# A rewritten last mixer and five smaller edits at the seams of a two-block transformer kernel (one core)

## The reference

```python
# first block, twice: feed-forward, mixer, feed-forward (272 rows: 16 meta tokens and 256 tokens)
def token_mixer(h, ...):
    fq, fk, fv, ff, gq, gk, gv, ga, gr, g_merge_a, g_merge_b = jnp.split(h @ w_in, points, axis=-1)
    o_fox = fox_attention(heads(fq), heads(fk), heads(fv), log_f, key_valid)      # 8 heads of 64
    log_a = log_sigmoid(ga @ w_alpha_up + b_alpha) * (valid / 16)
    o_gla = gla_chunked(heads(gq) / 8, heads(gk), heads(gv), heads(log_a))        # 4 heads
    o_gla = rmsnorm(o_gla, g_gla_out) * silu(gr)
    y = sigmoid(g_merge_a) * (o_fox @ w_fox_o) + sigmoid(g_merge_b) * (o_gla @ w_gla_o)
    return y @ w_out
# after the first block only the 256 tokens go on: first_block returns h[:, BLOCK:]

# second block: ffn, mlstm_mixer, ffn; k_sh, v_sh; ffn, dilated_mixer, ffn
def dilated_mixer(h, mem_n, k_sh, v_sh, w_q, q_gain, w_out, rel_bias, w_mem_kv, ...):
    p = h @ w_q                                            # 12 heads of 64, and 4 memory heads
    q_d = rms_norm(heads(p[..., :768]), q_gain)
    for g, (window, dilation) in enumerate(((128, 1), (512, 4), (2048, 16))):   # 4 heads in each
        s = q_d[g] @ k_sh[g].T / 8 + bias[bucket of distance]; causal, in dilated windows
        outs[g], lses[g] = softmax(s) @ v_sh[g], log of the sum
    h_d = outs * softmax(lses over the three groups)
    h_m = memory_cross_attention(p[..., 768:], mem_n, w_mem_kv, ...)   # 4 heads, 256 memory rows
    return concatenate([h_d, h_m]) @ w_out
# feed-forward: x + 0.5 * ((silu(n @ w_gate) * (n @ w_up)) @ w_down), n = rms_norm(x)
```

## Time and profile before

| | us |
|---|---|
| median of 3 runs | 2573.98 (2571.54 to 2575.33) |
| the profiled execution, its time | 2574.36 |
| its span from first to last instruction | 2573.0 |
| PE busy | 2448.4 (95%), mean granted clock 0.967 |
| DVE busy | 1676.7 (65%) |
| ACT busy | 1246.6 (48%) |
| DMA | 385.85 MB, mean 150 GB/s |

### The profile page before, as it was taken

One profiled execution on the slowest core, in us unless ns is written; L12 is line 12 of the kernel. 1 busy time (PEld: TensorE's weight loads), 2 busy tenths in 40 slices (PEclk: granted clock), 3 DMA queues, 4 the chain that ended last, 5 costly groups with the idle time before them and its releaser, 6 DMA issues.

```text
span 2573.0 us, 45875 instructions
## 1 busy us (share of the span) xinstructions
PE 2448.4 (95%) x18769; PEld 2322.9 (90%) x18769; DVE 1676.7 (65%) x3006; ACT 1246.6 (48%) x2099; POOL 33.6 (1%) x63
## 2 busy tenths in 40 slices
PE   7999999999999989999999998999999999769999
PEld 6999788899999977899999998989998999457999
DVE  5656777776575487778648846756656765455664
ACT  5444455554354445556445634645445644334542
POOL 2000000000000000000000000000000000000000
PEclk9999999999999999999999998989999999677999
DMA  7655433565465453346655653427655665412653
GB/s 193 174 179 141 117 91 109 141 182 176 148 178 175 158 132 99 99 137 189 189 183 162 183 176 102 119 58 191 185 184 157 180 189 171 127 41 83 180 181 140
DMA packets 589729, 385.85 MB, mean 150 GB/s; under 512 B 44587, under 2 KB 564111, under 8 KB 589392
## 3 DMA queue, kind: packets, MB, share of 16 engines
q1 hardware_dynamic: 585408, 374.00, 50.5%
q10 hardware_dynamic: 2336, 5.92, 0.6%
q0 software_dynamic: 1776, 2.98, 0.4%
HBM read 378.59 MB, written 4.19 MB: 149 GB/s over the span
## 4 chain that ended last, share of the span: by engine, by line
PE 87%; DVE 8%; ACT 2%; issue 1%; DMA 1%; ACTq 0%; DVEq 0%
PE bank L516 86%; DVE wlo L1906 2%; DVE ry L1925 1%; DVE ry L1923 1%; PE bank L825 0%; ACT whi L1243 0%; DVE smh L2357 0%; DVE rst L1927 0%; PE bank L601 0%; ACT rst L1264 0%; DMA xs<-in_x 0%; PE bank L1163 0%; ACT rst L1266 0%; DMA wraw<-in_w_ffn_gu 0%; DVE ssb L2677 0%
## 5 line engine op out<-in xcount | busy, mean ns | idle before, releaser
L1906 DVE TENSOR_TENSOR wlo<-wraw,whi 128x1024 fp32r<-128x1024 f32 (+2 forms) x723 | 866.7, 1205 | 290.7 <-ACT whi L1243 287.3
L1243 ACT ACTIVATE whi<-wraw 128x1024 fp32r<-128x1024 f32 (+2 forms) x723 | 746.9, 1042 | 596.5 <-DMA wraw<-in_w_ffn_gu 175.2
L516 PE MATMUL bank<-xhi,whi 128*128 128x256 f32 (+2 forms) x4024 | 606.6, 291 | 40.7 <-ACT xhi L1279 24.6
L516 PE MATMUL bank<-xhi,wlo 128*128 128x256 f32 (+2 forms) x4024 | 592.8, 287 | 11.4 <-DVE wlo L1906 11.4
L516 PEld LDWEIGHTS bank<-xhi,whi 128*128 128x128 f32 (+1 forms) x4024 | 535.4, 190 | 63.0 <-ACT xhi L1279 27.1
L516 PE MATMUL bank<-xlo,whi 128*128 128x256 f32 (+2 forms) x4024 | 581.4, 285 | 0.0
L516 PEld LDWEIGHTS bank<-xhi,wlo 128*128 128x128 f32 (+1 forms) x4024 | 535.5, 190 | 15.4 <-DVE wlo L1906 15.1
L516 PEld LDWEIGHTS bank<-xlo,whi 128*128 128x128 f32 (+1 forms) x4024 | 528.2, 188 | 0.2
L516 PE MATMUL bank<-act_hi,wlo 128*128 128x256 f32 (+1 forms) x1408 | 400.5, 284 | 0.0
L516 PE MATMUL bank<-act_lo,whi 128*128 128x256 f32 (+1 forms) x1408 | 400.1, 284 | 0.0
L516 PE MATMUL bank<-act_hi,whi 128*128 128x256 f32 (+1 forms) x1408 | 399.1, 283 | 0.0
(11 more groups left out here) (396 smaller groups left out, 1815.9 us busy)
## 6 DMA issues: line engine op xcount, KB each, us to landing
wraw<-in_w_ffn_gu SPq DMA_DIRECT2D x176, 512.0 KB, 3.9
wraw<-in_w_ffn_down SPq DMA_DIRECT2D x88, 512.0 KB, 3.2
wraw<-in_ffn_w_gate SPq DMA_DIRECT2D x88, 512.0 KB, 3.9
wraw<-in_ffn_w_up SPq DMA_DIRECT2D x88, 512.0 KB, 3.9
...
```

Source lines behind the costliest of these rows:

```text
L516: return E.matmul(out_, lhsT, rhs, start=first, stop=last, skip_group_check=True)
L1243: A.activation(flat(whi, u), flat(wraw, u), ACT.Copy).then_inc(S("hi"), 1)
L1906: V.tensor_tensor(flat(wlo, u), flat(wraw, u), flat(whi, u).bitcast(F32), ALU.subtract).then_inc(lo_ready[u % RING], 1)
```

## The change

1. **Fourth slab's low part**: DVE makes the wlo of the next stage's fourth slab before the additions of the last two tiles, in ffn 4, 5 and 6 and in the last mixer.
2. **Banks**: slabs 7 to 20 of mixer1 take banks 0, 1, 4, 5 in turn (`MIX_BANKS`) instead of 0 and 1; mixer2a has 6 banks of its own for its first slabs instead of 4, and its first cell step moves from step 5 to 6.
3. **Second layer's columns**: in mixer1(1), fq, gr, ma and the fo and go products are done for the 256 token columns alone, and `fox` has 16 units (queries 16 to 143 over 144 keys, 144 to 271 over 272) instead of 24.
4. **Gate bias on ACT**: ACT adds `b_alpha` as it reads the bank (Identity with bias), where DVE did; the factor 1/16 moves from a DVE multiplication into the scale of ACT's exponentials.
5. **shared_kv**: ffn 6's first `xhi` waits for the second pass of the last kv slab, not for ffn 6's own first slab.
6. **Last mixer rewritten**: the bias rows are 3 matmuls of 4x512 inside ffn 6 (steps 4, 6, 8) and 3 writes of 8 KB; the 12 reads of `bias` (128 KB each, POOL's queue, now with an overlapping source) are issued there too, and so are the memory operands `b_mp` (steps 12 to 19). Queries of the dilated heads are stored with each 128 columns reversed, which fits the reads' order; the values' operand is turned back by the product below. Slabs: 4 in the head, then bq and mkv slabs mixed; norms trail by two steps; one dilated unit per step from step 4, one memory unit per step from step 10. PE no longer transposes DVE's scaled probabilities: it multiplies the unscaled ones by a diagonal matrix that ACT makes of 1/den (`dgb`, `dgm`). The first 6 of 8 channel tiles of the first 4 output slabs are done in steps 15 to 18 while memory units run, the rest after.

```diff
+GATE_TEMP = 16.0
+MIX_FIRST, MIX_WIDE = 7, 21
+MIX_BANKS = [i if i < MIX_FIRST else (0, 1, 4, 5)[(i - MIX_FIRST) % 4] if i < MIX_WIDE else i % 2 for i in range(41)]
+B_HEAD = [("bq", 0, s) for s in (0, 2, 4, 1)]
+B_ORDER = [("bq", 0, 3), ("bq", 0, 5), ("mkv", 1, 0), ("bq", 0, 6), ("mkv", 1, 1), ("bq", 0, 7), ("mkv", 1, 2), ("mkv", 1, 3)]
+B_UNIT_STEP, B_MEM_STEP, B_TURN_STEP = 4, 10, 11
+B_IDLE, B_EARLY = 5, 4
+B_ROW_AT = (4, 6, 8)
...
-            src = IN["scratch"][h].rearrange("p u -> (p u)")[0:P * 511].rearrange("(p u) -> p u", u=511)[:, 127:127 + T]
-            G.dma_start(bias[:, h, :], src).then_inc(S("bias_in"), 16)
+            row = IN["scratch"][h, 0:1, :]
+            G.dma_start(bias[:, h, :], bass.AP(row.tensor, row.offset, [[1, P], [1, T]])).then_inc(S("bias_in"), 16)
...
 # PE, ffn
+                if F == 6 and j in B_ROW_AT:
...
+                    mm(bank[6][0:4, :], tab[0:BUCKETS + 1, 4 * g:4 * g + 4], ohb[0:BUCKETS + 1, 512 * g:512 * g + 512], True, True).then_inc(S("b_row"), 1)
 # PE, mixer1
-                    project((name, L, s), x)
+                    project((name, L, s), xq if name == "fq" else x)
 # PE, last mixer
+            def dilated():
+                for n in range(B_UNITS_N + 3):
+                    while c.step < B_UNIT_STEP + n:
+                        yield
+                    if n < B_UNITS_N:
+                        h, i, rows, t0, W = b_unit(n)
+                        E.wait_ge(S("hn_out"), hn0 + (3, 6)[h // 2])
+                        if n > 0:
+                            E.wait_ge(S("b_sb"), n)
+                        for g, s in enumerate(b_scores(W)):
+                            m = mm(s, b_q[rows, 2 * g + h // 2, t0:t0 + P], k_sh[rows, 2 * g + h // 2, 0:W], True, True)
+                        m.then_inc(S("b_s"), 1)
+                    if 0 <= n - 3 < B_UNITS_N:
...
+                                m = mm(b_outs(g)[rows, t0:t0 + P], v_sh[:, k, (4 * g + h) * HD:(4 * g + h) * HD + HD],
+                                       pt[:, (g * ns + k) * P:(g * ns + k) * P + P], k == 0, k == ns - 1)
+                    if 0 <= n - 2 < B_UNITS_N:
+                        h, i, rows, t0, W = b_unit(n - 2)
+                        E.wait_ge(S("b_d"), n - 1)
+                        if n - 2 > 0:
+                            E.wait_ge(S("b_c"), n - 2)
+                        for q in range(3 * (i + 1)):
+                            o = bank[2][:, q * P:q * P + P] if q < 4 else bank[6][:, (q - 4) * P:(q - 3) * P]
+                            m = mm(o, PPb[(n - 2) % 3][:, q * P:q * P + P], dgb[(n - 2) % 2], True, True)
 # ACT, last mixer
+                        A.activation(dgb[z], C("flip"), ACT.Copy, scale=stat_a[:, 4 * z + 3:4 * z + 4]).then_inc(S("b_d"), 1)
 # DVE, end of an ffn of the second block
                     if nxt is not None:
                         if d == 3:
                             lo_until(X + 3)
+                        if d == 5:
+                            lo_until(X + HEAD)
                         if d > 0:
                             fill_low(nxt, cols2, d - 1)
 # DVE, mixer1
-                            own(V.tensor_scalar(cb[:, q, :], bank[2 + q][:, 0:T1], gain1[:, 96 + 2 * L + q:97 + 2 * L + q], None, ALU.add))
...
-                            own(V.tensor_scalar(z, z, 1.0 / 16.0, None, ALU.mult))
```

More of the change, by code:

```diff
@@ L584, in next_bank @@
             i = c.proj - c.first
-            if i >= c.banks + 2:
+            if c.banks == MIX_FIRST:
+                before = [j for j in range(i) if MIX_BANKS[j] == MIX_BANKS[i]]
+                if before:
+                    E.wait_ge(S("evac"), c.first + before[-1] + 1)
+            elif i >= c.banks + 2:
                 E.wait_ge(S("evac"), c.proj - 1)
@@ L1123, in project_b @@
[L1123 to L1145 removed]
+            xm = lambda k, part: b_mp[part][:, k, :]
@@ new lines, in mixer2b @@
+            xo = lambda k, part: hd[part][:, k, :] if k < 6 else b_hm[part][:, k - 6, :]
+            hn0, tv0 = c.hn, c.tv
+            def main():
+                head_projects(B_HEAD, x, FILL["b"])
+                stat(cols2, 7)
+                yield
+                for i, key in enumerate(B_ORDER, HEAD):
+                    if key[0] == "mkv":
+                        E.wait_ge(S("mp_lo"), 2 * KD)
+                    if i >= HEAD + 2:
+                        E.wait_ge(S("evac"), c.proj - 1)
+                    c.proj += 1
+                    products(b_bank(i)[:, 0:T], AT[key], slab_cols(AT[key], 0, P), xm if key[0] == "mkv" else x).then_inc(S("used"), 1)
+                    yield
+                for _ in range(B_IDLE):
+                    yield
+                E.wait_ge(S("b_out"), 6)
+                for d in range(B_EARLY):
+                    u = AT["bo", 0, d]
+                    products(bank[d][:, 0:T], u, slab_cols(u, 0, P), xo, n_k=6, last=False)
+                    yield
+                yield
+                yield
@@ new lines, in norms @@
+            def norms():
+                for n in range(len(B_NORMS)):
+                    while c.step < B_NORM_AT[n]:
+                        yield
+                    E.wait_ge(S("hn_sq"), hn0 + n + 1)
+                    if n == 0:
+                        E.wait_ge(S("evac"), c.first + HEAD)
+                    if B_NORM_AFTER[n] > 0:
+                        E.wait_ge(S("hn_out"), hn0 + B_NORM_AFTER[n])
+                    mm(b_norm_bank(n), C("mean64"), bsq[:, n % 6, :], True, True).then_inc(S("hn_ms"), 1)
+                    c.hn += 1
@@ L1183, in mixer2b @@
+            weave(main(), [norms(), turns(), dilated(), memory()], c)
             E.wait_ge(S("mem_o"), 4)
-            E.wait_ge(S("evac"), c.proj)
             for d in range(KD):
                 u = AT["bo", 0, d]
-                if d >= 4:
-                    wait_h(E, H_OF_FILL["f7"], d - 4)
-                products(bank[4 + d % 4][:, 0:T], u, slab_cols(u, 0, P),
-                         lambda k, part: hd[part][:, k, :] if k < 6 else b_hm[part][:, k - 6, :]).then_inc(S("used"), 1)
+                if d < B_EARLY:
+                    products(bank[d][:, 0:T], u, slab_cols(u, 0, P), xo, n_k=2, first=False, k0=6).then_inc(S("used"), 1)
+                else:
+                    products(bank[d][:, 0:T], u, slab_cols(u, 0, P), xo).then_inc(S("used"), 1)
@@ L1416, in main @@
                     if i == 1:
+                        for q in range(2):
+                            A.wait_ge(S("wau"), 2 * L + q + 1)
+                            A.activation(cb[:, q, :], bank[2 + q][:, 0:T1], ACT.Identity, bias=gain1[:, 96 + 2 * L + q:97 + 2 * L + q]).then_inc(S("cb"), 1)
                         log_sigmoid(ssum[:, :])
@@ L1858, in mixer2b, with squares_of @@
+            def squares_of():
+                for i in range(HEAD, len(B_NORMS)):
+                    while c.step < i - 2:
+                        yield
+                    square(i)
+            weave(main(), [norms(), squares_of(), turns(), dilated(), memory()], c)
+            c.proj += 12
             for d in range(KD):
@@ new lines, in memory @@
+            def memory():
+                for i in range(MEM_N + 3):
+                    while c.step < B_MEM_STEP + i:
+                        yield
+                    if 0 <= i - 1 < MEM_N:
+                        z = (i - 1) % 2
+                        V.wait_ge(S("mem_e"), MEM_N + i)
+                        V.reciprocal(stat_b[:, 4 * z + 3:4 * z + 4], stat_b[:, 4 * z + 2:4 * z + 3]).then_inc(S("mem_r"), 1)
+                    if i < MEM_N:
+                        mx, nm = (stat_b[:, 4 * (i % 2) + y:4 * (i % 2) + y + 1] for y in range(2))
+                        V.wait_ge(S("mem_s"), MEM_N + i + 1)
+                        own(V.reduce_max(mx, bank[4][:, 0:T], AX_X))
+                        wait_own()
+                        V.tensor_scalar(nm, mx, -1.0, None, ALU.mult).then_inc(S("mem_nm"), 1)
+                    if 0 <= i - 3 < MEM_N:
+                        pair, tl, t0, n, h, hh = MEM_UNITS[i - 3]
+                        if tl == 1 and hh == 1:
+                            to_lo(b_hm[1][:, pair, :], bank[7][:, 0:T], b_hm[0][:, pair, :], "mem_oh", 2 + pair + 1).then_inc(S("mem_o"), 1)
@@ L2697, in mixer2b @@
+            weave(main(), [norms(), dilated(), memory()], c)
             for d in range(KD):
                 ahead(("bo", 0, d))
-                add_out(d, ("bo", 0, d), "f7", 4 + d % 4)
+                if d == KD - 1:
+                    lo_until(AT["g", 7, 0] + HEAD)
+                add_out(d, ("bo", 0, d), "f7")
             fill_low("f7", cols2, KD - 1)
```

761 lines of the change are left out of this document (361 added, 400 removed).

## The result

| | us |
|---|---|
| before, median of 4 runs | 2574.15 (2571.54 to 2575.33) |
| after, median of 4 runs | 2491.62 (2486.05 to 2493.38) |
| ratio | 0.9677, 95% interval 0.966 to 0.9694 |
| after, the profiled execution | 2486.05 (span 2484.7), granted clock 0.983 (before 0.967) |

The kernel is 83 us faster.

The account below looks back on a forecast made before the run. PE bounds the feed-forward stages; the last mixer is a chain across engines, costing PE idle time and clock. Terms −60.6 + 2.7 − 7.1 − 6.2 − 4.2 − 3 − 0.5 = −78.9 from 2574.4 gave 2495 us, range 2474 to 2523.

Parts of the forecast that it names:

- The last mixer at full clock: 112: Last mixer: 109.5 us of PE work plus 2.5 of waits, 112 in place of 190.6.
- My count of 5.5 to 5.9 us per step: Last mixer: DVE's work in a step with a wide unit, against 7.3 us of PE work, so DVE has slack.
- The clock: +18: Last mixer: clock loss of 6 us in steps with slabs, 11 in five without, 1 in early output; 130 in all.
- The rival of a full clock: Last mixer: the clock comes back fully because PE no longer idles; stage 112, kernel 2477 us; chance 0.20.
- Bias rows in ffn 6: +2.7: ffn 6: three bias-row matmuls at 0.90 us each add 2.7 us to PE, the bound there.
- Low parts: −7.1: Seams at mixer2a, shared_kv and ffn 7: wlo waits of 1.64 and 1.89 us go, plus 1.7 of clock dip.
- 256 columns and fox: −10.4: mixer1(1): 768 matmuls on fewer columns save 6.2 us, fewer fox units 4.2.
- Banks: −3: mixer1: of 4.3 us of waits a layer only 2.0 can be had; saves 1 in the first layer, 2 in the second.
- mixer2a: −0.5: mixer2a: six banks remove a wait of 3.3 us, mostly taken up by what follows; bounds −3 and +3.
- Bias reads, shared_kv's fill: 0: ffn 6: the 12 bias reads stay hidden, with 130 us to spare; shared_kv: one earlier xhi behind a busy PE saves 0.
- the rival of a slower kernel: Last mixer: the first unit waits for the 12 bias reads, landing 79 us later than needed; chance 0.03.
- the 0.65 to 0.9: Last mixer, new steps 4 to 14: a granted clock outside this range would show the prediction wrong.

Follow-up runs that it names:

- twobanks: The changed kernel with banks 0 and 1 alone for slabs 7 to 20 of mixer1; median 2487.89 us, ratio 0.9667.
- turns: The changed kernel with 96 unused 128x128 transposes added back to back in ffn 6; 2499.61 us, one run.
- rows33: The changed kernel with 12 unused float32 matmuls of 512 columns, 33 rows deep, on ones and a one-hot tile, added in ffn 6; 2505.97 us, one run.
- deep33: The changed kernel with 12 unused float32 matmuls of 512 columns, 33 rows deep, on the memory tile, added in ffn 6; 2507.95 us, one run.
- deep128: The changed kernel with 12 unused float32 matmuls of 512 columns, 128 rows deep, on the memory tile, added in ffn 6; 2499.61 us, one run.
- lateturn: The changed kernel with memory units from step 15 instead of 10, behind the dilated units, and five more empty steps; 2502.83 us, ratio 0.9738.
- noearly: The changed kernel with the four early output products done behind the memory units instead of between them; 2495.32 us, ratio 0.9711.
- turn: The changed kernel with the last mixer's 52 diagonal products replaced by transposes of unscaled probabilities, 1/den and query reversal left out; 2484.61 us, ratio 0.9667.
- oldlow: The changed kernel with the fourth slab's low part behind the additions again at all four seams; 2493.72 us, ratio 0.9695.
- cols272: The changed kernel with mixer1's second layer computed for all 272 columns and 24 units again, last product still 256 columns; 2496.96 us, ratio 0.9707.
- abanks4: The changed kernel with mixer2a's 4 own banks and first cell step at 5, as before; 2487.29 us, ratio 0.9669.

## Why the prediction held, and where its terms were off

The range held and the forecast, 2495, is 3.4 us above the median. That closeness is in part luck. The sum was built on one trace, and against the changed kernel's trace it is 9.4 us too high: 2495.5 for 2486.05. By stages it priced the last mixer 10.7 too long, mixer2a 2.7 and mixer1(0) 1.2, and mixer1(1) 3.4 too short, the rest 1.8. The 10.7 are the clock (12.9 too much) and the work (2.1 too much), less waits (4.3 too few).

- **The last mixer at full clock: 112.** It was 119.3 with the clock's loss in it. Waits: 6.8 instead of the 2.5 I added; the two for b_q (3.0) lie where DVE was busy 12.96 of 14.70 us: norms, evacuations and low parts of the first steps pile up there. The one for b_km (1.2) comes later, in steps where DVE was busy 17.45 of 23.10. My count of 5.5 to 5.9 us per step took a step in the middle; at the start DVE has three norms in one step. The clock's loss, from the windows: 1.2 + 2.3 + 1.6 = 5.1. What is left is 107.4 of work, 109.5 in the forecast.
- **The clock: +18, the step that failed.** Measured +5.1. Of the 18, the 6 for the steps with slabs was about right: all 5.1 lie there and in the norms just ahead of them. I priced the five steps without slabs at 0.65 from the old bias and memory stretches, +11, and the early output steps at +1; both cost nothing, and the five steps ran 21.80 us at 1.00. In the nine traces with this code they take 21.8 to 24.4, and in two of them the clock is not full:

```profile
2233.88:2258.26 24.38, 22.76 (x144) 17.72 (x143) 12.74 (x42) 13.63 (x42) 0.00 (x0) 0.93 0.02 6
```

  That is twobanks (turns is the same): behind a wait of 1.51 for ssb the clock is 0.58 from 2238 to 2242, and 1.00 in the rest, so the stretch is not near 0.65 there either. The rows of before were read rightly, but "float32 matmuls" as such was not their cause. In the bias rows it was the depth of 33 rows (rows33, deep33 against deep128). In the memory stretch the clock fell behind waits of 1.94 and 0.64 for ppb and then stayed at 0.50 from 2330 to 2348.5, up to the output slabs, although PE was busy 17.40 of these 18.50 us. For 10 of them it had no idle time at all:

```profile
2334.00:2344.00 10.00, 10.00 (x28) 5.10 (x28) 4.22 (x16) 2.90 (x10) 0.00 (x0) 0.50 0.00 1
```

  lateturn shows the same with diagonal products in place of transposes, 0.50 from 2262 to 2271.8; noearly, with waits of up to 1.28 among its memory units, keeps 1.00. So memory units alone held a full clock (noearly) and did not bring a fallen one back, where the dilated units of lateturn and twobanks did. Why is open, and no run has memory units alone with transposes. The rival of a full clock, since PE no longer idles, described the second half of the stage rightly, though its time, 2477, is 14.6 under the median. The rule of the Trainium skill (TensorE: Matmul & The Clock Gate, Part 4: PE-mode transpose) that stands beside it in the prediction did not hold: transposes keep the clock as well (turn, turns).
- **Bias rows in ffn 6: +2.7.** Measured +3.4 for the stage, three times 0.95 and the rest not assigned.
- **Low parts: −7.1 and the last mixer's −1.89.** oldlow has 9.4 by stages, 6 to 11 with the scatter of traces, ffn 7's clock dip included; 4.4 us of 11.4 in wlo waits stay, none over 0.7.
- **256 columns and fox: −10.4.** Shown by cols272, 8.2 to 10.1.
- **Banks: −3.** Nothing that shows (twobanks). I had seen that gd is late next, and still counted 2.0 of 4.3 from the gap between 949.08 and 951.04. With the waits for qa gone PE comes to gd at 942.2 and stands there until 946.2, behind the evacuations and low parts in DVE's queue; with them back it comes when the operand is ready, and the layer is as long.
- **mixer2a: −0.5.** −2.0 to −2.7 by the traces (abanks4), half of it clock that the forecast did not count; the time can't show it.
- **Bias reads, shared_kv's fill: 0.** No wait of PE names either; nothing came of the rival of a slower kernel.

Of what the changed profile was to show, three things did not come: mixer1(1) with its output products is 9 us shorter and not 13, one wait for b_q is 1.9, and the clock from 2199.2 to 2255.4, steps 4 to 14, is 0.93 in the mean (1.00 from 2233.6), above the 0.65 to 0.9 that the prediction named as its own sign of being wrong. So its time held, and its account of the clock did not.
